# Part of the sums of squares behind three residual norms made from expanded sums while the branch tiles come in, and the chunk order of the three seams turned

## The reference

```python
def rms_norm(x, g):
    xf = x.astype(jnp.float32)
    y = xf * lax.rsqrt(jnp.mean(xf * xf, axis=-1, keepdims=True) + EPS)
    return (y * g.astype(jnp.float32)).astype(x.dtype)

    h = h + 0.5 * rms_norm(swiglu(rms_norm(h, ffn1_pre_g), ...), ffn1_post_g)
    u = rms_norm(h, mix_pre_g);  proj = u @ w_in
    ...
    h = h + rms_norm(merged @ w_out, mix_post_g)
    h = h + 0.5 * rms_norm(swiglu(rms_norm(h, ffn2_pre_g), ...), ffn2_post_g)
    ple_gate = jax.nn.sigmoid(rms_norm(h, ple_pre_g) @ w_ple_gate)
    h = h + rms_norm(ple_gate * (p @ w_ple_proj), ple_post_g)
```

## Times and profile before

| | us |
|---|---|
| median of three timed runs | 1917.85 (1917.04 to 1919.11) |
| the profiled execution's own time | 1916.6 |
| its span in the trace | 1914.5 |
| PE busy | 1827.7 (95%), 8444 matmuls |
| DVE busy | 1104.1 (58%) |
| ACT busy | 660.9 (35%) |
| POOL busy | 174.9 (9%) |
| mean granted TensorE clock | 0.985 |

### The profile page before, as it was taken

The page is one execution under the profiler, slowest core; times in us unless marked ns, Lnnn a source line. Parts: engine busy times, 40 slices in busy tenths (PEclk is TensorE's granted clock), DMA queues, the critical chain, the costliest instruction groups (busy, mean ns, idle before and its releaser), DMA issues.

```text
span 1914.5 us, 23688 instructions
## 1 busy us (share of the span) xinstructions
PE 1827.7 (95%) x8444; PEld 1483.3 (77%) x8444; DVE 1104.1 (58%) x1666; ACT 660.9 (35%) x1003; POOL 174.9 (9%) x125
## 2 busy tenths in 40 slices
PE   6999999999999999999999989999898999999985
PEld 4677888888888888888776767789676888888874
DVE  6665588887435645532353776586766655542266
ACT  5333332332323222222233234564543322222242
POOL 1231000000000000000023334433000000000000
PEclk9999999999999999999999989999999999999997
DMA  4677332223322222332212233131441222232211
GB/s 155 61 84 43 101 108 97 91 97 109 106 82 88 90 96 99 103 106 91 97 68 71 99 121 132 56 121 56 127 137 67 99 97 90 98 124 93 92 66 55
DMA packets 55460, 180.63 MB, mean 94 GB/s; under 512 B 6336, under 2 KB 7104, under 8 KB 55392
## 3 DMA queue, kind: packets, MB, share of 16 engines
q1 hardware_dynamic: 43344, 157.33, 24.4%
q10 hardware_dynamic: 12048, 22.40, 7.5%
HBM read 167.65 MB, written 12.06 MB: 94 GB/s over the span
## 4 chain that ended last, share of the span: by engine, by line
PE 80%; DVE 11%; DMA 3%; ACT 3%; issue 2%; ACTq 0%; POOL 0%; SPq 0%; DVEq 0%
PE bank L781 20%; PE bank L782 20%; PE bank L783 20%; PE bank L803 2%; PE bank L805 2%; PE bank L804 2%; DMA raw<-in_w_proj 2%; PE bank L877 2%; DVE score L2336 2%; PE bank L878 1%; PE bank L879 1%; DVE best L2335 1%; PE bank L852 1%; PE bank L819 1%; DVE chunk L1991 1%
## 5 line engine op out<-in xcount | busy, mean ns | idle before, releaser
L1283 ACT ACTIVATE w_hi<-raw 128x1024 fp32r<-128x1024 f32 (+2 forms) x281 | 304.4, 1087 | 734.5 <-PE bank L783 627.5
L781 PE MATMUL bank<-a_hi,w_hi 128*128 128x512 f32 x1256 | 494.2, 393 | 11.1 <-DVE w_lo L1894 3.8
L783 PE MATMUL bank<-a_hi,w_lo 128*128 128x512 f32 x1256 | 490.3, 390 | 0.0
L782 PE MATMUL bank<-a_lo,w_hi 128*128 128x512 f32 x1256 | 490.3, 390 | 0.0
L1894 DVE TENSOR_TENSOR w_lo<-raw,w_hi 128x1024 fp32r<-128x1024 f32 (+2 forms) x222 | 284.1, 1280 | 255.5 <-ACT w_hi L1283 242.1
L781 PEld LDWEIGHTS bank<-a_hi,w_hi 128*128 128x128 f32 x1256 | 236.8, 189 | 72.6 <-issue 17.8
L783 PEld LDWEIGHTS bank<-a_hi,w_lo 128*128 128x128 f32 x1256 | 236.6, 188 | 49.8
L782 PEld LDWEIGHTS bank<-a_lo,w_hi 128*128 128x128 f32 x1256 | 236.8, 189 | 48.1
L781 PE MATMUL bank<-h_hi,w_hi 128*128 128x512 f32 x568 | 221.0, 389 | 0.0
L782 PE MATMUL bank<-h_lo,w_hi 128*128 128x512 f32 x568 | 221.0, 389 | 0.0
L783 PE MATMUL bank<-h_hi,w_lo 128*128 128x512 f32 x568 | 220.9, 389 | 0.0
(11 more groups left out here) (306 smaller groups left out, 2159.7 us busy)
## 6 DMA issues: line engine op xcount, KB each, us to landing
raw<-in_w_up SPq DMA_DIRECT2D x132, 512.0 KB, 3.4
raw<-in_w_down SPq DMA_DIRECT2D x48, 704.0 KB, 4.0
raw<-in_w_proj SPq DMA_DIRECT2D x59, 512.0 KB, 3.5
raw<-in_w_wo SPq DMA_DIRECT2D x8, 512.0 KB, 4.2
raw<-in_w_branch SPq DMA_DIRECT2D x16, 256.0 KB, 2.8
gates_in<-spill ACTq DMA_DIRECT2D x16, 256.0 KB, 3.2
raw<-in_w_out SPq DMA_DIRECT2D x8, 512.0 KB, 3.5
raw<-in_w_ple SPq DMA_DIRECT2D x8, 512.0 KB, 3.5
```

Source lines behind the costliest of these rows:

```text
L781: mm(dst[:, :], wh, hi[:, k, :], start=(first and c == 0), stop=False)
L782: mm(dst[:, :], wh, lo[:, k, :], start=False, stop=False)
L783: step = mm(dst[:, :], wl, hi[:, k, :], start=False, stop=(last and c == n - 1))
L1283: fn(w_hi[:, slot, 0:size], raw[:, slot, 0:size], ACT.Copy).then_inc(unit_high, 1)
```

## The change

(a + b)^2 = a^2 + 2ab + b^2. The new stream is x' = x + y g r, where r is the branch's factor, one number per token. Its sum of squares is the sum of x^2, plus 2 r times the sum of x y g, plus r^2 times the sum of (y g)^2. The three sums don't need r. For chunks 0 to 5 (`EXPANDED`) they are made while the branch's tiles come in: DVE multiplies `y` g by `x` and adds it to `cross`, ACT squares `y` with the gain as scale and DVE adds that too; behind `down2` the square of `x` is done as well, and later seams carry the stream's sum over in `stream_sum`. Chunks 6 and 7 keep their squares in the seam and now go first (`SEAM`). PE sums the parts over the partitions (`sum_parts`), and `fold_sums` puts them together on DVE, behind the fifth chunk of the seam. `sum_x` of the stream norm moves to behind the fourth chunk, and ACT's root to behind the sixth. The waits that the weights' order needs are adapted (`tile_part`).

```diff
+AFTER = {"mixpre": "post1", "pre2": "postmix", "plepre": "post2"}
+SEAM = (6, 7, 0, 1, 2, 3, 4, 5)
+EXPANDED = range(6)
...
+        sums = {"pre1": val, "post1_branch": silu, "postmix_branch": silu, "post2_branch": rstd, "post1_stream": gate}
+        crosses = {"post1": val, "postmix": val, "post2": diagonal}
+        stream_sum, folding = small[:, 20:24], small[:, 28:32]
...
+            def sum_parts(split):
+                name, dst = AFTER[split], parts_bank(split)
+                n = tuple(AFTER).index(split)
+                pe.wait_ge(cross_added, DC * n + len(EXPANDED))
+                sum_columns(crosses[name], 0, dst=dst)
+                pe.wait_ge(sum_added, square_at(name + "_branch", EXPANDED[-1]) + 1)
+                step = sum_columns(sums[name + "_branch"], QB, dst=dst)
+                if name == "post1":
+                    pe.wait_ge(sum_added, square_at("post1_stream", EXPANDED[-1]) + 1)
+                    step = sum_columns(sums["post1_stream"], 2 * QB, dst=dst)
+                step.then_inc(parts_ready, 1)
...
@@ first_three, first_tiles
+                    if split in AFTER and k == 3:
+                        sum_x(split)
...
-                if not summed:
+                if not summed and split not in AFTER:
                     sum_x(split)
...
@@ PE, behind down2
             total_x("post1")
-
-            pe.wait_ge(const2_loaded, 16 * 3)
             for i in range(AUX_BANKS):
                 wait(tile_read("up2", i))
+            sum_parts("mixpre")
+
+            pe.wait_ge(const2_loaded, 16 * 3)
...
             total_x("postmix")
+            wait(tile_read("out", 5))
+            sum_parts("pre2")
...
                 if i == 2:
                     sum_x("post2")
+                    wait(tile_read("up3", 0))
+                    sum_parts("plepre")
                 if i == 4:
                     spread("post2")
...
@@ ACT, scaled_highs
-                for k in range(DC):
-                    act.wait_ge(x_ready, before + k + 1)
+                for at, k in enumerate(SEAM):
+                    act.wait_ge(x_ready, before + at + 1)
                     scaled_high(g, k)
-                    square(stage, k, x[:, k, :], (x_ready, before + k + 1))
-                    if k == 3:
+                    if k not in EXPANDED:
+                        square(stage, k, x[:, k, :], (x_ready, before + at + 1))
+                    if at == 3:
                         unit_high_part(UNIT[units][0] + 3)
-                take_root(stage, D)
+                    if at == 5:
+                        take_folded_root(stage)
...
@@ ACT, keep_branch
                     fn(y[:, k, :], tile_bank(stage, k)[:, :], ACT.Copy).then_inc(tile_sem(stage, k), 1)
+                    if k in EXPANDED:
+                        square(square_stage + "_branch", k, y[:, k, :], tile_read(stage, k), prm(g, k))
+                        if square_stage == "post1":
+                            square("post1_stream", k, x[:, k, :], (x_ready, DC))
...
@@ DVE
+            def fold_sums(split):
+
+                parts, r = parts_bank(split), inverse[:, 0:QB]
+                dve.wait_ge(parts_ready, 1 + tuple(AFTER).index(split))
+                step(v.tensor_tensor(folding, parts[:, QB:2 * QB], r, ALU.mult))
+                step(v.scalar_tensor_tensor(folding, parts[:, 0:QB], 2.0, folding, ALU.mult, ALU.add))
+                step(v.tensor_tensor(folding, folding, r, ALU.mult))
+                before = parts[:, 2 * QB:3 * QB] if split == "mixpre" else stream_sum
+                step(v.tensor_tensor(stream_sum, folding, before, ALU.add))
+                dve.wait_ge(total_ready, SUM[split] + 1)
+                v.scalar_tensor_tensor(folded, stream_sum, 0.0, stat_bank[:, 0:QB], ALU.max, ALU.add).then_inc(
+                    folded_ready, 1)
...
@@ DVE, add_branch
-                    if k and split:
-                        add_square(split[0], k - 1)
-                    if k < DC and split:
+                    if at and split and order[at - 1] not in EXPANDED:
+                        add_square(split[0], order[at - 1])
+                    if at < DC and split:
                         scaled_low(split[0], split[1], k)
-                    if k in units:
-                        split_unit(units[k])
+                    if at in units:
+                        split_unit(units[at])
+                    if at == 4 and split:
+                        fold_sums(split[0])
...
@@ DVE, branch_kept
+                    if k in EXPANDED:
+                        wait(tile_read(stage, k))
+                        step(v.scalar_tensor_tensor(chunk[:, k % 2, :], y[:, k, :], prm(g, k), x[:, k, :], ALU.mult,
+                                                    ALU.mult))
+                        if k == 0:
+                            v.tensor_copy(cross[:, :], chunk[:, 0, :]).then_inc(cross_added, 1)
+                        else:
+                            dve.wait_ge(cross_added, n + k)
+                            v.tensor_tensor(cross[:, :], cross[:, :], chunk[:, k % 2, :], ALU.add).then_inc(
+                                cross_added, 1)
+                        add_square(square_stage + "_branch", k)
+                        if square_stage == "post1":
+                            add_square("post1_stream", k)
```

More of the change, by code:

```diff
@@ L862, in total_x, with tile_part, part @@
                 spread(name)
-            def first_three(stage, split, hi=a_hi, lo=a_lo):
[L869 to L881, removed]
+            def tile_part(stage, split, i, at, hi=a_hi, lo=a_lo):
+                first, k = UNIT[stage][0], chunks_of(split)[at]
+                if at == 0:
+                    wait_bank(stage, i)
+                    pe.wait_ge(unit_split, first + i + 1)
+                dst, cols = tile_bank(stage, i), slice(k * P, (k + 1) * P)
+                wh, wl = w_hi[:, (first + i) % SLOTS, cols], w_lo[:, (first + i) % SLOTS, cols]
+                mm(dst[:, :], wh, hi[:, k, :], start=(at == 0), stop=False)
+                mm(dst[:, :], wh, lo[:, k, :], start=False, stop=False)
+                step = mm(dst[:, :], wl, hi[:, k, :], start=False, stop=(at == DC - 1))
+                if at == DC - 1:
+                    step.then_inc(unit_done, 1)
+            def first_three(stage, split, hi=a_hi, lo=a_lo):
+                def part(i, at):
+                    tile_part(stage, split, i, at, hi, lo)
                 if split in BY_TILE:
@@ L908, in first_tiles @@
                 first_three(stage, split)
-                if not summed:
+                if not summed and split not in AFTER:
                     sum_x(split)
                 done = DC - FOURTH_FROM if split in FOURTH else 0
-                fill(stage, [(3, done, done + (DC - done) // 2)])
+                half = done + (DC - done) // 2
+                for at in range(done, half):
+                    tile_part(stage, split, 3, at)
                 spread(split)
-                fill(stage, [(3, done + (DC - done) // 2, DC)])
+                for at in range(half, DC):
+                    tile_part(stage, split, 3, at)
             def folded_tiles(stage):
@@ L1319, in take_root, with take_folded_root @@
                     root_ready, 1)
+            def take_folded_root(split):
+                act.wait_ge(folded_ready, 2 + tuple(AFTER).index(split))
+                fn(root[:, 0:QB], folded, ACT.Sqrt, bias=prm("eps"), scale=1.0 / D).then_inc(root_ready, 1)
             def load_root_table():
@@ L1541, in _ @@
             load_root_table()
-            keep_branch("down2", "post1")
+            keep_branch("down2", "post1", "ffn1_post_g")
             take_root("post1", D)
```

85 lines of the change are left out of this document (52 added, 33 removed).

## The result

The changed kernel takes 1924.87 us, the median of seven runs (1920.35 to 1931.44); the kernel before took 1919.11 beside it (seven runs). The ratio is 1.0029 [1.0018, 1.0040]: about 5.5 us slower. A second set of twelve runs gave 1924.15 (ratio 1.0027 [1.0019, 1.0036]). The forecast was 1921.0, within 1916.0 to 1925.5. The profiled execution took 1925.71 us, span 1923.9, clock 0.981.

The account below looks back on a forecast made before the run. PE was taken to bound steady stretches, so only its waits in the three seams could be won; seam terms of +0.5, 0 and +2.7 made +3.2 us on 1917.85, forecast as 1921.0 us, range 1916.0 to 1925.5.

Parts of the forecast that it names:

- the squares lay in the shadow of `a_hi`: In the seams, DVE's square add runs while `a_lo` waits for ACT's 0.73 us `a_hi`, so removing it gains nothing.
- Squares removed, 0: Six of eight adds on DVE and six squares on ACT leave each seam: 0 us gained.
- the pace of 2.93 us: In all seams, `chunk` would still follow `chunk` by 2.93 us with no square between.
- the wait for `a_hi`: In the seams, DVE's wait would grow from 0.19 to about 0.9 us.
- The fold, 0.9 us a seam: Five small DVE instructions behind each seam's fifth chunk delay the next `chunk`: 0.9 us a seam.
- `sum_x` moved, -0.9: Its one-column matmuls leave each seam's tail for PE's wait for chunks: -0.9 us a seam.
- First seam, +0.5: Fold +0.9, `sum_x` -0.9, and 0.5 given back where PE waits for the square of `ckv_raw`: +0.5 us.
- Second seam with what follows, 0: Second seam: the fold's 0.9 us and the moved `sum_x`'s -0.9 cancel to 0.
- Third seam, `sum_parts` +1.6: Two column-sum sets on PE between `sum_x` and `pproj` tile 2 put off `spread`: +1.6 us.
- Third seam, the wait in the fold, +1.1: The fold waits for PE's total of the two remaining squares, PE being late at half clock: +1.1 us.
- The sum: All three seams together: +0.5, 0 and +2.7, total +3.2 us.
- the rival of the clock: PE's clock falls in the widened wait before the sixth chunk: one fall about 1923, two 1925 us; chance 0.18.

Follow-up runs that it names:

- e9: The kernel before without six of the eight squares and adds of each seam, nothing in their place (norm values wrong): 1919.54 us, ratio 1.0000.
- e12: The changed kernel run once more, unaltered, as control: 1924.15 us, ratio 1.0027 to the kernel before.
- e1: The changed kernel with `fold_sums` and ACT's root moved behind the last chunk of the seam: 1920.14 us, ratio 1.0002 to the kernel before.
- e5: The changed kernel with eight spare matmuls filling PE's wait ahead of the sixth chunk in the first two seams: 1923.73 us, ratio 1.0029 to the kernel before.
- e6: The changed kernel without the new sums in the branch stages, PE's column sums kept (norm values wrong): 1925.51 us, ratio 1.0038 to the kernel before.
- e7: The changed kernel with each seam chunk's `a_lo` issued on DVE one chunk late: 1925.32 us, ratio 1.0034 to the kernel before.
- e11: The changed kernel with only the third seam's `sum_parts` moved behind the `pproj` tiles: 1920.09 us, ratio 1.0007 to the kernel before.

## Why the prediction held, point by point

The range held, and the two main readings with it: the squares lay in the shadow of `a_hi`, and the fold and `sum_parts` cost what their steps take. That the sum came near is in part luck: one term was too large and two losses that it had put at nothing stood against it. The time itself came 3.9 us above the forecast. Of that, 1.3 is the kernel before, whose median beside it was 1919.11 and not 1917.85, some 1.7 goes with the lower clock, and the rest is the terms below.

- **Squares removed, 0:** right, and shown by e9. So were the pace of 2.93 us and the wait for `a_hi`: about 0.9 was forecast, 0.79 came.
- **The fold, 0.9 us a seam:** 0.86 measured. The steps stand 0.19 to 0.20 us apart, as in the earlier trace rows.
- **`sum_x` moved, -0.9:** the stretch behind the second seam is 0.85 us shorter in the changed kernel (342.52 to 341.67), and 0.8 to 1.0 in every kernel that moves it.
- **First seam, +0.5:** +0.35 in the first profile, -0.08 up to the stream factor and +0.43 behind it, where the wait for the square of `ckv_raw` is, 0.55 us long; the kernel before has none there. e12 had +1.51, with the fall of the clock.
- **Second seam with what follows, 0:** +1.64 and -0.85, so +0.8. This is the term that was too small, and not for the reason that I had allowed 0.5 us for, column sums that overrun PE's wait. Here the clock falls sooner, inside `spread`, which ends 2.19 us behind the reciprocal and not 1.39:

```profile
1456.72 1.06 PE L890 MATMUL bank<-ident,inverse 128*128 128x128 f32 x4
1457.57 1.71 PE L845 MATMUL bank<-ones,val 128*128 128x1 f32 x8
1459.14 1.85 PE L845 MATMUL bank<-ones,silu 128*128 128x1 f32 x8
1461.30 0.77 PE L910 MATMUL bank<-a_hi,w_hi 128*128 128x512 f32 x1 [0.32 <-issue]
```

  So the first `chunk` comes 2.23 us behind the reciprocal (1.43 before), and all others are late by that 0.8; the fold's 0.86 makes up the rest. A set takes 1.6 to 1.85 us here, not 0.8, but both end in time: the first matmul starts 1.14 us behind the start of `a_lo`, and 1.12 before. In first seams, where there are three sets, they do overrun, by 0.3 us in the first profile and by 1.3 in e1 and e5; PE's wait ahead of the sixth chunk takes that up. In e6 `spread` runs at full clock and its second seam is longer only by the fold and one fall of the clock behind it: the sets cost 0, as forecast. Five profiles of six with the fold in the middle show 10.2 us of half clock at this seam's start (after, e5, e7, e11, e12; e6 6.8), against one in four of the kernels that come from the one before, and none of the four with the fold at the end. Why it falls sooner stays open.
- **Third seam, `sum_parts` +1.6:** 1.78 (5.26 less 3.48 from reciprocal to first chunk), confirmed by e11 with 1.79.
- **Third seam, the wait in the fold, +1.1:** this term was too large. This wait exists in the first profile, with the releaser I named, but is 0.45 us, and e5, e6, e11 and e12 have none:

```profile
1857.11 0.16 DVE L2051 TENSOR_TENSOR small<-small 128x4 f32<-128x4 f32 x1
1857.72 0.16 DVE L2053 SCALAR_TENSOR_TENSOR small<-small,bank 128x4 f32<-128x4 f32 x1 [0.45 <-PE bank L845]
1857.83 0.75 DVE L2069 SCALAR_TENSOR_TENSOR chunk<-y,par,rstd 128x512 f32<-128x512 f32 x1
```

  The seam as a whole was forecast at +2.7 and came at +2.90, which is luck: 1.8 for `sum_parts`, 0.86 and 0.45 for the fold, -0.9 for `sum_x`, and 0.7 that no term held. DVE's third `a_lo` waits 2.10 us for ACT in this profile (1.35 before, 1.29 in e12), since the `w_hi` ahead of ACT's `a_hi` waits longer for the DMA of a `w_ple` unit. In e5, e6 and e12 the seam is +1.7, and the half clock in it 3.4 us long, not 6.8.
- **The sum:** forecast +3.2; seams and stretch behind them +4.0 in the first profile, +3.8 in e12, +2.9 in e5; 3.8 at equal clock. The mechanism was right and its size 0.6 us short: the second seam took 0.8 more than its 0, the wait in the fold 0.6 to 1.1 less. The rest of the 5.5 is clock, most of it outside the seams, where no term of mine stood; the rival of the clock had it in the widened wait alone.

## What to carry to other kernels

Work in the shadow of a round trip between two engines is free, and taking it away buys nothing until the round trip itself is gone: look at what the engine waits for behind the instruction to be removed. First let the engine run one item ahead, then remove the work; here 0 and 3.0 us became 13.4 (0, 0.7 and 11.7 at equal clock). And compare the granted clock before a difference of a few us is explained. A short chain of small steps belongs behind the last item of such a loop, above all when one of its steps waits for the engine that is being fed.

## What was not expected of the hardware

- In e7 a wait of DVE for PE and one of PE for DVE stood back to back (1.57 and 2.42 us), with 3.4 us of half clock behind them, and took back nearly all of a gain that is 9.9 us without them.
- A wait of the same length on PE (2.59 us) is followed by full clock in one execution and by 3.4 us of half clock in another of the same kernel, for 1.2 us. At this place that happened behind four of nine waits of 2.4 us or more, and behind none of eleven of 1.8 us or less.
- A set of one-column f32 matmuls (8 instructions) goes from 0.8 us to 1.6 to 1.85 us at half clock: work that fits a wait at full clock can overrun it by 1.3 us (e1, e5). Here that cost nothing, because PE waits again later.
